# Gate logits' matmuls of a mixing step: eight pieces of 3 to 5 parts in place of twelve of 1 to 4

## What is computed

```python
h = rmsnorm(x, norm_mix_g)
p = h @ w_in                      # latents | rwkv columns z | gate_logits (2 * 1024 columns)
o_a = chunk_causal_attention(...) # branch A
o_b, wkv_new, shift_new = rwkv7_time_mix(z, ...)   # branch B, a recurrence over the rows
gates = sigmoid(gate_logits).reshape(B, L, 2, 1024)
x = x + sum(gates * (branches @ w_out))
x = x + hier_moe(rmsnorm(x))
```

## Time and profile before

| | busy us, share of the span |
|---|---|
| TensorE, matmul | 1499.6 (91%) |
| TensorE, weight load | 1064.4 (65%) |
| VectorE | 861.3 (52%) |
| ScalarE | 445.4 (27%) |
| GpSimd | 102.2 (6%) |

### The profile page before, as it was taken

One profiled execution on the slowest core, in us unless ns is written; L12 is line 12 of the kernel. 1 busy time (PEld: TensorE's weight loads), 2 busy tenths in 40 slices (PEclk: granted clock), 3 DMA queues, 4 the chain that ended last, 5 costly groups with the idle time before them and its releaser, 6 DMA issues. The chain is left out here.

```text
span 1646.0 us, 38768 instructions
## 1 busy us (share of the span) xinstructions
PE 1499.6 (91%) x16352; PEld 1064.4 (65%) x16352; DVE 861.3 (52%) x1874; ACT 445.4 (27%) x882; POOL 102.2 (6%) x102
## 2 busy tenths in 40 slices
PE   4999999969999999999999599988998699999894
PEld 3888888854566666666667366653554577776663
DVE  3454455555656676676776566664776223222111
ACT  2222222223222332332231144434444111111110
POOL 0000000000000000000000000000000122333321
PEclk9999999989999999999999699999999699999998
DMA  8432221525232223112112424437953699999962
GB/s 320 147 123 90 89 96 64 193 93 179 77 123 75 81 82 105 59 70 83 59 46 73 115 64 95 96 79 260 373 192 141 234 330 343 342 351 361 336 236 35
DMA packets 101326, 259.55 MB, mean 158 GB/s; under 512 B 34240, under 2 KB 53328, under 8 KB 91824
## 3 DMA queue, kind: packets, MB, share of 16 engines
q1 hardware_dynamic: 93424, 239.92, 42.7%
q0 software_dynamic: 7744, 17.33, 4.5%
HBM read 205.32 MB, written 60.56 MB: 162 GB/s over the span
## 5 line engine op out<-in xcount | busy, mean ns | idle before, releaser
L527 PEld LDWEIGHTS a_ps<-a_hT,a_wz 128*128 128x128 f32 x1792 | 202.6, 192 | 3.8 <-issue 3.8
L527 PE MATMUL a_ps<-a_hT,a_wz 128*128 128x128 f32 x1792 | 204.0, 275 | 0.0
L1927 PE MATMUL d_ps<-late,last_down 128*128 128x512 f32 x256 | 115.4, 598 | 1.5 <-DVE last_down L1691 0.8
L2095 DVE COPY f_xT<-f_turned 128x384 f32<-128x384 f32 x32 | 17.9, 558 | 154.5 <-PE f_turned L2062 154.5
L1927 PEld LDWEIGHTS d_ps<-late,last_down 128*128 128x128 f32 x256 | 46.7, 190 | 51.5 <-issue 50.2
L2289 DVE TENSOR_SCALAR f_y<-f_down,table 96x512 f32<-96x512 f32 x32 | 23.9, 747 | 99.7 <-PE f_down L2088 86.0
L1453 ACT ACTIVATE late<-c_score,c_top 128x1024 f32<-128x1024 f32 (+8 forms) x72 | 50.6, 703 | 93.0 <-DVE c_top L1402 92.5
L1101 PE MATMUL b_ps<-r_wg,r_hT 128*128 128x512 f32 x128 | 64.5, 637 | 12.0 <-POOL b_S L759 10.0
L821 DVE TENSOR_TENSOR b_M<-b_ps,r_causal 128x512 f32<-128x512 f32 x72 | 46.4, 686 | 54.8 <-PE b_ps L1162 54.3
L2296 ACT ACTIVATE f_xT<-f_turned 128x384 f32<-128x384 f32 x32 | 15.7, 491 | 190.4 <-PE f_turned L2062 190.4
L1101 PE MATMUL b_ps<-b_wg,b_hT 128*128 128x512 f32 x128 | 63.3, 616 | 0.9 <-DMA b_hT<-hT_d 0.9
(11 more groups left out here) (369 smaller groups left out, 2907.9 us busy)
## 6 DMA issues: line engine op xcount, KB each, us to landing
wgu<-w_gate_up SPq DMA_DIRECT2D x17, 2048.0 KB
late<-w_gate_up SPq DMA_DIRECT2D x10, 2048.0 KB
wd<-w_down SPq DMA_DIRECT2D x17, 1024.0 KB
last_up<-w_gate_up SPq DMA_DIRECT2D x5, 2048.0 KB
late<-w_down SPq DMA_DIRECT2D x10, 1024.0 KB
r_hT<-hT_d SPq DMA_DIRECT2D x18, 512.0 KB, 4.3
b_hT<-hT_d SPq DMA_DIRECT2D x18, 512.0 KB, 4.1
gate_d<-b_logits SPq DMA_DIRECT2D x32, 256.0 KB, 2.6
```

What stands on the lines that cost most here:

```text
L527: mm = pe.matmul(banks[Z_BANKS[n % 2]][:, j * P:(j + 1) * P], wz[:, i, (g + j) * P:(g + j + 1) * P], hT[t % 2][:, i, :], start=(i == 0), s ...
L1927: mm = pe.matmul(banks[2 + u][:], oT[t % 2][:, HB * branch(u) + k, :], wo[:, HB * branch(u) + k, half(u)], start=(k == 0), stop=(k == HB - 1))
```

## The change

One line. The counts of parts by slot, 28 in each step in both kernels:

```diff
-        FILL_OF = (2, 2, 3, 2, 3, 2, 3, 4, 2, 1, 2, 2)
+        FILL_OF = (3, 0, 0, 4, 0, 0, 5, 4, 3, 3, 3, 3)
```

## The result

The changed kernel took 1658.27 us (median of 6 runs, 1652.56 to 1663.23), the one before 1650.6 (median of 6). The ratio is 1.0052, 95% interval 1.0037 to 1.0067: **slower by about 8 us**, where I forecast 5.3 us less. The profiled execution took 1658.18 us; its span is 1656.0 for 1646.0, its mean granted clock 0.958 for 0.967.

The account below looks back on a forecast made before the run. It took TensorE, 91% busy, as the bound. Steps 1 to 7 -9.5, step 0 +2.9, activations +0.2 and step 8 +1.1 gave -5.3 us, so 1645.7 us from the median; range 1641 to 1652.5.

Parts of the forecast that it names:

- steps 2 to 7: Full steps of the stage: each shorter by -0.96 for switches and -0.43 for a wait, with +0.03 for lost cover.
- Step 8: Last step of the stage: moved decode parts and waits for VectorE make it +1.1 us longer, between 0.5 and 1.5.
- step 1: Second step of the stage: a full step's gain, less +0.5 us for an early wait for hT.
- step 0: First step: new waits for VectorE cost +2.9 us net; a fall of the clock moves there at the same length.
- The pieces: Each full step: four pieces fewer on TensorE save shape switches, -0.96 us a step, between -0.86 and -1.06.
- `merge` to lora: Full steps: going straight from 64*64 to 64*128 wins between 0 and -0.2 us, taken as -0.1.
- The wait of slot 11: Last `merge` of a full step: a third part ahead of it removes its wait for VectorE, -0.43 us.
- The cover that is gone, in full steps: Slots 1 to 5: less TensorE work hides VectorE; a tie at slot 6's `low`, charged 0.03 us a step.
- Rival (d): Slots 4 and 5: VectorE's chain sets the time instead of TensorE, at the worst 1656 us; chance 0.07.
- All is passed on: Behind the stage: the chain of waits passes on the whole gain; no transfer starts at a fixed time.
- (b): Step 0: the median runs before had no clock episode, only the new kernel has; -2.0 us, 1649.0, chance 0.20.
- The activations: Waits for hT at unit seams: -0.3 us in step 3, +0.5 in step 1, none in step 5; sum +0.2.

Follow-up runs that it names:

- e7: The kernel before with one edit of the change in each of steps 2, 4, 6 and 7, run once for its profile: 1648.88 us.
- e3: The kernel before with the changed counts in steps 2 to 7 only: 1641.41 us, ratio 0.9954 to the kernel before.
- e11: The kernel before with step 0 changed and three unread wide matmuls added in its slot 5: 1653.52 us, ratio 1.0022 to the kernel before.
- e1: The changed kernel with step 8's parts put back as before: 1651.37 us, ratio 1.0012 to the kernel before.
- e5: The changed kernel with two unread wide matmuls added in slot 1 of step 8: 1651.95 us, ratio 1.0020 to the kernel before.
- e6: The changed kernel with three unread wide matmuls added in slot 5 of step 0: 1651.90 us, ratio 1.0018 to the kernel before.
- e9: The kernel before with the changed counts in step 0 only: 1655.19 us, ratio 1.0038 to the kernel before.
- e10: The kernel before with the changed counts in step 1 only: 1656.25 us, ratio 1.0041 to the kernel before.
- e12: As e10, but slot 0's third part, which asks early for hT, moved to slot 3: 1648.30 us, ratio 0.9991 to the kernel before.
- e4: The kernel before with the changed counts in step 8 only: 1657.56 us, ratio 1.0039 to the kernel before.
- e2: The changed kernel with steps 0 and 1 put back as before: 1648.44 us, ratio 0.9990 to the kernel before.
- e8: The kernel with own counts for steps 0, 1, 3, 5 and 8, changed counts elsewhere: 1634.40 us, ratio 0.9912 to the kernel before.

## Why the prediction was wrong

By the two profiles steps 2 to 7 came out as forecast, to 0.5 us. Step 8 was 6.5 us off (+7.6 for +1.1), step 1 was 5.0 us off (+4.1 for -0.9) and step 0 1.7 us (+4.6 for +2.9). Term by term:

- **The pieces**, -0.96 a step with -0.86 and -1.06 as bounds: right. The steps 2, 4 and 6 are 1.33 shorter; less 0.43 for slot 11's wait that is 0.90, between the two. The middle value for `merge` to lora was a wrong guess: the row shows no gain (1.05, 2.18). With no gain there my step would have been -1.26; -1.33 was measured, since the pieces cost a little more than 0.19 (e7: 0.20 to 0.32). The Trainium skill ("TensorEngine Tiling (Array Packing)", Key Properties) says that a change of tiling mode drains the engine; the row agrees.
- **The wait of slot 11**, -0.43: right, L1247 is gone from the waits, and e7's step 7 has it together with one piece (57.91, 0.62 less).
- **The cover that is gone, in full steps**: right, the tie of 6.09 us held without a wait. Rival (d) has no row for it: step 7's 6.31 is `outputs`, not VectorE.
- **All is passed on**: right (e3).
- **Step 0**, +2.9: the waits are right (0.53, 0.53 and 3.32, with 3.39 forecast), and so are the +2.9 at one clock (e11: some 3, as above) and the fall at the long one. Wrong is that the first fall goes away for good: with 0.74 us of idle for 1.60 ahead of the first `low` the clock still fell in the changed kernel, for 3.4 us in place of 6.8, and in e1, e5 and e6; in e9 and e11, with the same counts in step 0, it did not. With the old counts it fell in all seven traces, so (b), no episode before the change, isn't borne out. The step lost 4.6 in the profiled pair, 3.3 in e9's profiled execution and 6 in e9's runs.
- **The activations**, +0.2: wrong in step 1, where I took 0.5 out of "0 to 1.9" and left the upper end out of the bounds of the sum: with it they reach -2.3, where -3.5 stands. The -0.3 of step 3 came to about -0.2 (1.75 us of wait for 1.93). In the trace of before the load is issued at 468.23 and the decode item is through at 472.05; these loads land 3.6 to 5.6 us after their issue, so the wait was to be had from there as up to 1.8. In the changed kernel it is issued at 475.10, the decode item ends at 479.0, and the load lands at 480.9. Together with what else comes in step 1 (the wait put down to "issue", the clock) this is 7 us by e10 against the kernel before and 8 against e12; in the two profiles it is 2.0, and the rest isn't shown.
- **Step 8**, +1.1: **this is the step that failed most.** The waits are right, e5 gives 23.5 with the added work where I had 23.1. The clock is missing. I asked for it in step 0, where the changed order leaves 3.4 us of idle, and not here, where it leaves two times 0.5 us. In the kernel before there are two waits of this length too (0.53 to 887.05, 0.52 to 894.71), but they are 7.7 us apart, with the 1.9 us of the decode item's narrow matmuls (L1104, x64) and three more pieces of work between them, and the clock stays at 1.00 until 910. In the changed kernel half of the narrow matmuls have moved to slot 0 and half to slot 3, nothing but one `merge` is between the waits, and it falls. 6.4 us by e4; by e5, 6.1 of the step's 7.6.
- My rule for it, that a single wait of 1.93 us had no fall after it and so less has none, was wrong, and not only because those waits stand among 64*64 matmuls: the very wait of rows 8 has a fall at it in e10, e11 and e12. One execution without a fall told nothing about the next. What makes the clock fall in one and not in the other stays open; only step 8 shows no exception: there it fell in all four traces with the changed counts and no work added in that step (the changed kernel, e2, e4, e6). The Trainium skill ("TensorE: Matmul & The Clock Gate", What's actually happening) says that the clock is set by how busy the engine has been recently. Busy time in the profile's sense doesn't decide it here: TensorE is 16.00 of 16.00 us busy at 0.50.
- The medians differ by +7.7 where the sum of measured parts is: e3 -7.6, e4 +6.4, e9 +6.3, e10 +6.8, together +11.9. The rest of 4 us isn't explained; the scatter of steps 0 and 1 and the intervals (2.5 to 2.7 us to either side of each) are of that size. Taken by what undoing gives back, the sum closes better: 6.6 us (e1) and 10.2 us (e2) of loss less the 7.6 of e3 are +9.2, where the changed kernel's own ratio is +8.6.

## What to carry to other kernels

A distribution that wins in the steady steps has to be checked at the edges of the stage by itself, where the other work that hides it is missing: here six steps won 8 us and three lost 16. Work that is moved out of a stretch of small matmuls can take the clock with it, even where it leaves hardly a wait (step 8: two waits of 0.5 us, 6 us of loss); and one profile in which a wait left the clock alone doesn't show that it always will. Give the first and the last steps counts of their own. And where a double-buffered load is asked for, count the time from its issue to its first use at each seam, not only in the steady state.

## What the runs showed of the hardware that I had not expected

- In step 8 the granted clock stays at 0.50 for 17 us while TensorE is busy without a gap, most of it with tiled matmuls (64*64, 128*32, 128*64), in the changed kernel, e2, e4 and e6. It rose within the outputs of step 8 (L1211 and after, 128*64). Two wide matmuls of 1.9 us in all, put before the stretch and into its second wait, kept it at 1.00 (e5).
- It fell at the second of two waits of 0.53 and 0.52 us (e4) or up to 1.3 us behind it (e2). A single wait of 1.7 to 2.1 us in step 3, with the same work around it in all seven kernels, had a fall at it in three (e10, e11, e12) and none in four (before, e4, e7, e9).
- In step 0 it fell at the first waits in all seven traces with the old counts and in four of six with the changed ones. The runs of e6 and e5 spread over 15 and 22 us, those of e8 over 6; that falls of the clock in steps 0 and 1 are what spreads them is argued from the profiles, one for each kernel.
- A change of tile shape costs TensorE 0.16 to 0.20 us, an estimate from one change less and two less: a piece of the 128*128 parts costs 0.20 us beyond its matmuls between two other shapes, 0.32 where it parts two runs of 64*64 (e7, 58.54 less 58.34 and 58.22).
